# Neighbourhood attention of a hybrid mixer: position bands turned round once per head and added by VectorE, V products of two heads issued in alternation

## What is computed

```
scale = NA_DH ** -0.5                                   # q is scaled, 4 heads, width 64
bias = rpb[:, dr[:, None, :, None], dc[None, :, None, :]]   # by row and column distance
s_loc = einsum('bhrqd,bhrjkd->bhrqjk', qg, kb) + bias
s_loc = where(c_valid[:, None, :], s_loc, NEG_INF)
s_ctx = einsum('bhrqd,bhcd->bhrqc', qg, kc)
p = softmax(concat([s_loc, s_ctx]))
o = einsum('bhrqjk,bhrjkd->bhrqd', p_loc, vb) + einsum('bhrqc,bhcd->bhrqd', p_ctx, vc)
# context queries (layer 0 only): softmax(qc kc) vc, no bias
```

## Time and profile before

| | us |
|---|---|
| median of 3 runs | 2984.81 |
| lowest, highest | 2983.34, 2987.57 |
| the profiled execution | 2984.61 |
| its span | 2982.9 |
| PE busy | 2831.9 (95%) |
| DVE busy | 1709.3 (57%) |
| ACT busy | 853.5 (29%) |
| POOL busy | 289.7 (10%) |

### The profile page before, as it was taken

How to read it: one execution, slowest core, us unless ns; L and a number is a source line. 1 busy time by engine, 2 the same in 40 slices (tenths; PEclk the granted TensorE clock), 3 DMA queues, 4 the chain that set the end, 5 groups by cost and what they waited for, 6 DMA issues and landing times.

```text
span 2982.9 us, 39922 instructions
## 1 busy us (share of the span) xinstructions
PE 2831.9 (95%) x14770; PEld 2536.7 (85%) x14770; DVE 1709.3 (57%) x2888; ACT 853.5 (29%) x1145; POOL 289.7 (10%) x279
## 2 busy tenths in 40 slices
PE   6999999989988889999999899999998998899998
PEld 5999999979844679999999799999987843788887
DVE  7766667669636657666766762222247736633334
ACT  3221122241345442211221422112232256432222
POOL 0000000015222110000000100000004223100000
PEclk8999999999998899999999999999998999999999
DMA  5333233321211013333333232111212211123232
GB/s 205 102 130 132 95 132 126 122 72 54 57 38 46 29 49 120 136 111 113 114 140 105 71 120 74 54 63 63 73 48 93 68 33 41 57 92 103 87 105 78
DMA packets 63375, 264.95 MB, mean 89 GB/s; under 512 B 8880, under 2 KB 11824, under 8 KB 53680
## 3 DMA queue, kind: packets, MB, share of 16 engines
q1 hardware_dynamic: 50608, 180.17, 18.3%
q0 software_dynamic: 11520, 75.11, 7.7%
q10 hardware_dynamic: 1152, 8.39, 0.7%
HBM read 252.89 MB, written 2.10 MB: 85 GB/s over the span
## 4 chain that ended last, share of the span: by engine, by line
PE 83%; DVE 9%; ACT 4%; issue 2%; DMA 1%; POOL 0%; ACTq 0%; SPq 0%; DVEq 0%; POOLq 0%
PE ps L1512 76%; PE ps L1783 2%; DVE conv_acc L1247 2%; PE ps L1703 1%; DVE nmax L1353 1%; DVE w_lo L995 1%; PE ps L1732 1%; ACT e_sb L885 1%; PE ps L1711 1%; DVE rstd L1048 1%; ACT probs_t L899 1%; DMA x<-in_xT 1%; DVE mod_start_acc L1445 1%; DVE y_hi L1084 0%; DVE sq L1072 0%
## 5 line engine op out<-in xcount | busy, mean ns | idle before, releaser
L1512 PE MATMUL ps<-y_hi,w_hi 128*128 128x384 f32 (+2 forms) x3184 | 907.6, 348 | 70.0 <-DVE y_lo L1076 31.6
L1512 PE MATMUL ps<-y_hi,w_lo 128*128 128x384 f32 (+2 forms) x3184 | 896.1, 345 | 0.0
L1512 PE MATMUL ps<-y_lo,w_hi 128*128 128x384 f32 (+2 forms) x3184 | 895.4, 344 | 0.0
L1512 PEld LDWEIGHTS ps<-y_hi,w_hi 128*128 128x128 f32 x3184 | 583.8, 190 | 113.0 <-issue 42.1
L665 ACT ACTIVATE w_hi<-w_raw 128x1024 fp32r<-128x1024 f32 (+1 forms) x290 | 326.6, 1128 | 1037.4 <-PE ps L1512 1037.4
L1512 PEld LDWEIGHTS ps<-y_lo,w_hi 128*128 128x128 f32 x3184 | 587.7, 190 | 23.1
L1512 PEld LDWEIGHTS ps<-y_hi,w_lo 128*128 128x128 f32 x3184 | 586.9, 190 | 21.2 <-issue 0.5
L995 DVE TENSOR_TENSOR w_lo<-w_raw,w_hi 128x1024 fp32r<-128x1024 f32 (+1 forms) x290 | 386.3, 1333 | 306.5 <-ACT w_hi L665 303.1
L1010 DVE SCALAR_TENSOR_TENSOR mod_acc<-mod_raw,cact,mod_acc 128x256 f32<-128x256 f32 x896 | 360.0, 477 | 0.0
L1512 PE MATMUL ps<-h_hi,w_hi 128*128 128x384 f32 (+2 forms) x1254 | 354.1, 342 | 0.0
L1512 PE MATMUL ps<-h_lo,w_hi 128*128 128x384 f32 (+2 forms) x1254 | 351.5, 339 | 0.0
(11 more groups left out here) (167 smaller groups left out, 1976.5 us busy)
## 6 DMA issues: line engine op xcount, KB each, us to landing
w_raw<-in_w_up SPq DMA_DIRECT2D x176, 512.0 KB, 3.5
mod_raw<-in_w_mod POOLq DMA_DIRECT2D x64, 1024.0 KB, 5.1
w_raw<-in_w_down SPq DMA_DIRECT2D x64, 704.0 KB, 4.1
w_raw<-in_w_in SPq DMA_DIRECT2D x36, 512.0 KB, 3.4
mod_start<-in_w_mod ACTq DMA_DIRECT2D x8, 1024.0 KB, 22.1
w_raw<-in_w_out SPq DMA_DIRECT2D x16, 512.0 KB, 3.5
stack<-qk_hi SPq DMA_DIRECT2D x48, 96.0 KB, 2.1
band<-in_rpb POOLq DMA_DIRECT2D x16, 224.0 KB, 6.7
```

Source lines behind the costliest of these rows:

```text
L1512: mm = pe.matmul(slot[s][:, at:at + b - a], w[s][:, k, :], r[:, k, a:b], start=(opens and n == 0), stop=(closes and n == 2))
```

## The change

1. Steps: the neighbourhood heads go in pairs, (0, 1) and (2, 3). Within a pair the heads alternate: tiles (0, 1) of both, tiles (2, 3) of both, in layer 0 the context tiles of both.
2. Bands: PE no longer adds the band to the scores. It turns each head's band round once into `turn` or `outs` (896 columns, two matmuls per head; heads 0 and 1 ahead of the first scores, 2 and 3 after steps 1 and 2), and ScalarE, for head 1 VectorE, copies it back over the band. VectorE then adds 512 columns of it to each score slot in PSUM ahead of the maximum, and waits for its own addition.
3. V: for a pair of heads and 256 queries, PE issues per key block one matmul for the even head (upper rows of `outs`) and one for the odd head (lower rows). `value_jobs` lists these parts by step. Difference heads keep their 512-query products.
4. VectorE runs `maxima(k, 0)` ahead of `invert_sums(k - 1)`, in difference steps too. The order of the lambda products and the scaling of q (`rope_done`) is swapped.
5. The fourth band has a place of its own and is loaded and masked by POOL before the steps. `conv_pointwise` stands at steps 3 and 4 in both layers (before: 3 and 4, 2 and 3), the qk splits at steps 2 and 8 (before: 6 and 9, 5 and 8).

```diff
-    for h in range(HEADS):
-        tiles = [((0, 1), False), ((2, 3), False)] + [((0, 1), True)] * with_ctx
-        out += [("na", h, t, c, n == len(tiles) - 1) for n, (t, c) in enumerate(tiles)]
+    for pair in range(HEADS // 2):
+        for t, c in [((0, 1), False), ((2, 3), False)] + [((0, 1), True)] * with_ctx:
+            out += [("na", 2 * pair + odd, t, c, odd and t[0] == (0 if with_ctx else 2) and c == with_ctx) for odd in range(2)]
...
+CONV_STEP = 3
+SPLIT_STEPS = (2, 8)
+FLIP_STEPS = (1, 2)
+PAIR_PARTS = ((0, 2 * P, False), (2 * P, LAT, False), (LAT, TOK, True))
...
+def value_jobs(with_ctx):
+    jobs, at = [], 0
+    for pair in range(HEADS // 2):
+        for part in range(na_steps(with_ctx)):
+            at += 2
+            first = at + 2
+            if not jobs:
+                jobs.append(("na", pair, part, first + 1, 1))
+            else:
+                jobs.append(("na", pair, part, first, 1 if part == 2 else 2))
+    for h in range(HEADS):
+        at += LAT // P + with_ctx * (CTX // P)
+        jobs.append(("diff", h, 0, at + 2, 3 + with_ctx if h < HEADS - 1 else 1))
+    return jobs
...
-    bands.append(place("band3", [P, RPB_R - 1, GRID_W], at=at_free))
+    bands.append(place("band3", [P, RPB_R - 1, GRID_W], at=at_mod + 2 * chunk))
...
+                def flatten_band(h):
+                    act.wait_ge(sems["band_turned"], HEADS * layer + h + 1)
+                    act.activation(bands[h][:, :, :].rearrange("p r c -> p (r c)"),
+                                   (turn, None, turn, outs)[h][:, 0:(RPB_R - 1) * GRID_W], ACT.Copy).then_inc(sems["band_flat"], 1)
...
                 def maxima(k, s):
...
                     t.wait("scores")
+                    if kind == "na" and not ctx:
...
+                        j = GRID_H - 2 - 2 * tiles[s]
+                        dve.tensor_tensor(slot[s][:, 0:LAT], slot[s][:, 0:LAT],
+                                          bands[h][:, j:j + GRID_H, :].rearrange("p r c -> p (r c)"), ALU.add).then_inc(sems["biased"], 1)
+                        t.wait("biased")
                     dve.tensor_reduce(nmax[:, e:e + 1], slot[s][:, keys], AX_X, ALU.max,
...
                 for k in range(len(steps) + 3):
+                    if k < len(steps):
+                        maxima(k, 0)
                     if 1 <= k <= len(steps):
                         invert_sums(k - 1)
-                    if k < len(steps):
-                        maxima(k, 0)
...
+                def flip_band(h, into):
+                    t.wait("band_ready")
+                    n_band = (RPB_R - 1) * GRID_W
+                    for a, b in ((0, LAT), (LAT, n_band)):
+                        mm = pe.matmul(into[:, a:b], backward[:, :], bands[h][:, a // GRID_W:b // GRID_W, :], start=True, stop=True)
+                    mm.then_inc(sems["band_turned"], 1)
...
-                        j = GRID_H - 2 - 2 * tile
-                        mm = pe.matmul(slot[s][:, 0:LAT], backward[:, :], bands[h][:, j:j + GRID_H, :], start=False, stop=True)
...
+                def pair_values(pair, part, i, n_iter):
+                    a, b, of_ctx = PAIR_PARTS[part]
+                    keys = range(LAT // P if of_ctx else 0, TOK // P)
+                    share = len(keys) // n_iter
+                    for key in keys[share * i:share * (i + 1)]:
+                        for s in range(2):
+                            col = W + DH * (2 * pair + s)
+                            moving = ctx_probs[s][:, key - LAT // P, :] if of_ctx else probs_t[s][:, key, a:b]
+                            mm = pe.matmul(outs[DH * s:DH * s + DH, a:b], v_sb[:, key, col:col + DH], moving,
+                                           start=(key == keys[0]), stop=(key == keys[-1]))
```

More of the change, by code:

```diff
@@ L867, in mixer @@
                 step_tiles = []
[L868 to L870 removed]
+                jobs = value_jobs(with_ctx)
+                norm_at = None
+                copied_at, done = {}, {}
+                for n_job, (kind, h, part, first, n_iter) in enumerate(jobs):
+                    c = 6 + h if kind == "na" else 4 + h // 2
+                    copied_at = {at: chunk for at, chunk in copied_at.items() if chunk != c}
+                    copied_at[first + n_iter - 1] = c
+                    done[c] = n_job + 1
                 def copy_out(c):
[L873 removed]
+                    act.wait_ge(sems["pv"], jobs_before(layer) + done[c])
                     act.activation(mixed[c][:, 0:n], outs[:, 0:n], ACT.Copy).then_inc(sems["head_out"], 1)
@@ L886, in exponentials, with copy_probs @@
                                    accum_out=esum[:, e:e + 1]).then_inc(sems["exp"], 1)
-                def copy_probs(step, q):
-                    kind, h, tiles, ctx, last = step
-                    hn = head[0] % 2
+                def copy_probs(k, q):
+                    kind, h, tiles, ctx, last = steps[k - 2]
+                    hn = h % 2
                     t.wait("turned")
-                    if head[0] >= 2 or layer:
-                        act.wait_ge(sems["pv"], layer * 2 * HEADS + head[0] - 1)
+                    if jobs_before(layer) + jobs_by(with_ctx, k):
+                        act.wait_ge(sems["pv"], jobs_before(layer) + jobs_by(with_ctx, k))
                     if ctx:
@@ L1695, in scores @@
                     at = (LAT if ctx else 0) + P * tile
-                    band = kind == "na" and not ctx
                     for a, b in spans(TOK)[1 if ctx else 0:]:
@@ L1703, in scores @@
                             mm = pe.matmul(slot[s][:, a:b], z[rows, q, at:at + P], z[rows, key, a:b],
-                                           start=True, stop=not (band and a == 0))
-                    if band:
-                        if tile == 0:
-                            t.wait("band_ready")
-                        j = GRID_H - 2 - 2 * tile
-                        mm = pe.matmul(slot[s][:, 0:LAT], backward[:, :], bands[h][:, j:j + GRID_H, :], start=False, stop=True)
+                                           start=True, stop=True)
@@ new lines, in tiles_by @@
+                def tiles_by(k):
+                    return sum(len(step[2]) for step in steps[:max(k - 1, 0)])
+                def pair_values(pair, part, i, n_iter):
[8 more added lines that the diff above has]
+                                           start=(key == keys[0]), stop=(key == keys[-1]))
+                    if i == n_iter - 1:
+                        mm.then_inc(sems["pv"], 1)
@@ new lines, in head_values @@
+                def head_values(h, part, i, n_iter):
+                    rows = slice(DH * (h % 2), DH * (h % 2) + DH)
+                    products = [(key, False) for key in range(TOK // P)]
+                    products += [(key, True) for key in range(LAT // P, TOK // P)] * with_ctx
+                    share = -(-len(products) // n_iter)
+                    for key, of_ctx in products[share * i:share * (i + 1)]:
+                        if of_ctx:
+                            n_key = key - LAT // P
+                            mm = pe.matmul(outs[rows, LAT:TOK], v_sb[:, key, DH * h:DH * h + DH], ctx_probs[h % 2][:, n_key, :],
+                                           start=(n_key == 0), stop=(key == TOK // P - 1))
+                        else:
+                            mm = pe.matmul(outs[rows, 0:LAT], v_sb[:, key, DH * h:DH * h + DH], probs_t[h % 2][:, key, :],
+                                           start=(key == 0), stop=(key == TOK // P - 1))
+                    if i == n_iter - 1:
+                        mm.then_inc(sems["pv"], 1)
@@ new lines, in mixer @@
+                    for kind, h, part, first, n_iter in jobs:
+                        if first <= k < first + n_iter:
+                            if k == first:
+                                pe.wait_ge(sems["probs_t"], turned_before(layer) + tiles_by(first - 1))
+                                if part == 0 and (kind == "na" or h % 2 == 0):
+                                    t.wait("head_out" if kind == "diff" or h else "conv_out")
+                            (pair_values if kind == "na" else head_values)(h, part, k - first, n_iter)
+                            if kind == "diff" and h == 1 and k == first + n_iter - 1:
```

125 lines of the change are left out of this document (52 added, 73 removed).

## The result

| | median, us | runs | profiled execution |
|---|---|---|---|
| before | 2986.25 | 5 (2983.34 to 2996.69) | 2984.61 |
| after | 3007.65 | 5 (2999.52 to 3008.68) | 3008.68 |

The ratio after to before is 1.0051, 95% interval 1.0034 to 1.0068. The forecast was 2974 us with a range up to 2998: the sign was wrong and the time lies outside the range.

What follows compares the result with a forecast made beforehand. TensorE was taken to bound layer 1's second half, and the chain to the second transposes to bound whole steps afterwards. From 2984.6 us, -9.0 - 3.2 - 1.7 - 2.6 + 2.7 - 1 + 3 + 1 = -10.8 gave 2974, range 2960 to 2998.

Steps and rivals of the forecast that it cites:

- A pair of V calls: V products: two 256-column calls on different column halves run at once, 0.43 us a pair.
- the two rivals that priced it at 0.85 and more: V pairs: column halves one after the other, 2994 us, chance 0.17; array also drained at each alternation, 3007 us, chance 0.08.
- in turn: V pairs: column halves run one after the other, 0.85 us a pair, total 2994 us; chance 0.17.
- The addition: VectorE adding 512 band columns to scores in PSUM: 0.65 us, 0.70 with the wait behind it.
- Whole steps and the first difference steps: Whole step 7.49 us, layer 1's second half -3.2; first difference steps 4.84 (layer 0, -1.7) and 5.77 (layer 1, -2.6).
- Layer 0's second half, -9.0: Last neighbourhood steps of layer 0: walked step by step to 38.5 us from 47.5, a gain of 9.0.
- the clock takes it back: TensorE's waits lower its clock: five more slow stretches cost 12 us, total 2986 us; chance 0.12.
- First halves, +2.7 and -1: Early neighbourhood steps with convolution and pooling, counted and not walked: layer 0 loses 2.7 us, layer 1 gains 1.
- The term for turning the bands: First halves: TensorE turns four bands round per layer at 1.6 us each, +6.4, less 1.5 hidden in waits.
- VectorE's order, +3: 32 whole difference steps: loop of 3.97 us against 3.92, taken as 0.1 us lost each, +3.
- The rival priced it at 19 us: VectorE's new order exposes GpSimd's product in all 32 difference steps: +19 instead of +3, total 2990 us; chance 0.07.
- Band masks, +1, and the rope signal, 0: Mixer starts: two masks slow the convolution's centring, +1 us in all; moving the rope_done signal costs nothing.

Runs made afterwards that it cites:

- e1: Kernel after, with VectorE's reciprocal of the last step's sums ahead of the first maximum again in all 52 steps: 2998.43 us, ratio to before 1.0035.
- e9: e7 with the convolution's reciprocal moved to the end of step 1 and the first Q and K split to step 5: 2974.62 us, ratio to before 0.9951.
- e10: e9 with the turned bands and VectorE's additions put back: 2993.57 us, ratio to before 1.0014.
- e12: Kernel after, with VectorE's old order in the 32 difference steps alone: 2997.82 us, ratio to before 1.0033.
- e5: Kernel before, with only VectorE's new order added, in all 52 steps: 2999.22 us, ratio to before 1.0046.
- e4: Kernel after, with a pair's V products issued head after head instead of in turn: 3004.38 us, ratio to before 1.0056.
- e14: e12 plus one 512-column, 128-row product per score slot in the four whole steps of layer 0's second half: 2994.08 us, ratio to before 1.0026.
- e7: Kernel after, with bands added by TensorE and VectorE's old order again, leaving pairs and alternate V: 2984.40 us, ratio to before 0.9988.

## Why the prediction was wrong, point by point

- **A pair of V calls.** Right: 2.75 us for six pairs (859.23 to 861.97) is 0.46 each, forecast 0.43; the two rivals that priced it at 0.85 and more fall. The rule of the Trainium skill's "TensorE: Matmul & The Clock Gate", section "The mechanism", that a weight load overlaps a running product only where the row groups differ, does not hold here: twelve loads for the same rows fit into 1.45 us with their twelve products. The Trainium skill's "TensorEngine Tiling", section "Key Properties", that different tiles load and compute in parallel, agrees with the rows. But the rival "in turn" was also mis-sized: it is 0.64 a pair in threes, not 0.85.
- **The addition.** 0.70 us in 32 cases, forecast 0.65. Right. From its start to that of the maximum it is 0.73 (2467.58 to 2468.31), forecast 0.70.
- **Whole steps and the first difference steps.** 7.38 for 7.49; 4.84 for 4.84 (913.33 to 918.17 in layer 0), 5.71 for 5.77 (2482.28 to 2487.99 in layer 1). Right where the clock held. Where it fell in V, the step grew: 8.77 for 7.49, 5.66 for 4.84, 7.52 for 5.77. So layer 1's second half gave -2.1 for -3.2, and the first two difference steps -1.0 and -0.8 for -1.7 and -2.6.
- **Layer 0's second half, -9.0.** This step failed. The walk was made at the full clock, and the granted clock was 0.60. The rival "the clock takes it back" had the right mechanism and 0.12 of the chance, but mis-sized it: five short stretches, 12 us in all the stages (its own terms, 5 x 2.2, give 11). It was one stretch of 40 us, and this stage alone missed the forecast by 13 us (51.4 for 38.5), some 10 of them the clock's by e1.
- **First halves, +2.7 and -1.** Failed: +6.3 and +6.6. I counted products and additions and did not walk the order on VectorE. The term for turning the bands had the right price at the full clock (1.60), but four turnings took 7.8 us in layer 0 and 8.8 in layer 1 for 6.4, since part of them ran at the lower one. The later convolution, which the prediction named as a danger, is 5.39 us of waiting at 839.26, and e9 shows that moving one reciprocal and one split gives back 7.0 us in layer 0 and 2.0 in layer 1. e9 against e10 puts the turned bands with their copies and additions at 6.9 and 3.4 us above TensorE's band products there.
- **VectorE's order, +3.** Failed. The steady turn, from which I computed +0.05, became 0.13 shorter. I computed a turn with slack on VectorE and applied it to 32; the turns without slack, and the clock at the heads' ends, cost 6.1 us in layer 0 and 2.9 in layer 1 (e12 against after), of which the normalizing turns' 2.0 are surely the order's. The rival priced it at 19 us; these 9.0 and the 12 of e5's total lie between it and the forecast, and it charged the steady turns, which got shorter.
- **Band masks, +1, and the rope signal, 0.** Nothing shows a cost of them. GpSimd masked bands for 4.27 us from 804.82, and the centring of the convolution beside it took 1.94 at 807.77, as before. What lies outside the six stages is the same to 0.1 us in sum, but of three parts: 1.7 less ahead of the first mixer, 2.0 more between the two, 0.3 less behind. They weren't tried alone.

What stays open: which property of the work lets the clock fall. A 128-row product in each step held it at 0.92 or more in every profile here, and e4 with a longer V part had 0.88. But the extra product also shortens the wait in the step, from 1.32 to 0.46 in e14, so fuller use of the array and less waiting are not separated; a product of 64 rows of the same length wasn't tried. And the executions of one kernel differ in their mean clock, for no reason that the runs show.

## What to carry to other kernels

Work moved off the engine that bounds a stage pays only as long as that engine keeps its clock: with 0.97 us less per tile TensorE waited, fell to half speed and took longer for less work (51.4 us for 47.5). An order that is free in the steady loop has to be walked through the turns that carry extra work, since there the slack is gone. And what comes once per stage (a reciprocal of 5 us) goes where its engine is idle in the trace, not to the step that looks free on paper; here that move and the later split together were worth 10 to 11 us (e7 to e9), more than the pairs and alternate V had brought without them (2.6).

## What the runs showed of the hardware that I had not expected

- TensorE stayed at the lower clock for 40 us with no idle time to speak of (busy 38.6 of 40.0). Being busy did not bring it back.
- One more 512-column product per tile in four steps made their stage 6.4 us shorter (51.3 at 0.60; 44.9 with all eight products, 43.9 of it at 0.92).
- Products for the two column halves overlap without being issued alternately: 12 records in 1.93 us against 1.45, where three 512-column calls on one half took 2.72.
- Two VectorE multiplications of 768 columns took 1.82 us alone and 2.96 to 3.80 while GpSimd subtracted on 768 columns.
